# Keys and values of the context: made in the second layer's collecting stage instead of between its experts

## The reference

```python
def grouped_experts(xf, expert_id, gates, w_gu, w_down):
    ...
    def expert_block(args):
        xb, e = args
        a, b = jnp.split(xb @ w_gu[e], 2, axis=-1)
        return (jax.nn.silu(a) * b) @ w_down[e]
    ...
    return jax.ops.segment_sum(y_rows[dest] * w_sorted[:, None], tok_sorted, num_segments=T)
...
def c_mixer(u, uc, in_w, out_w, rpb, need_ctx):
    def proj(t):
        q, k, v, z = jnp.split(t @ in_w, 4, axis=-1)
        ...
    q, k, v, z = proj(u)            # 512 tokens
    q_c, k_c, v_c, z_c = proj(uc)   # 256 rows of context
    o = neighbourhood_latent(q, k, v, k_c, v_c, rpb)
    y = (o * jax.nn.silu(z)) @ out_w
```

## Time and profile before

| | us |
|---|---|
| median of 3 runs | 2964.3 (2963.15 to 2972.04) |
| the profiled execution, its own time | 2958.89 |
| its span, first to last instruction | 2957.1 |
| PE busy | 2686.4 (91%) |
| DVE / ACT / POOL busy | 1140.6 / 640.4 / 289.8 |
| second layer's experts, first to last product of PE | 1538.8 to 2054.5 |
| collecting stage, SP's first load to the next stage's first product | 2061.5 to 2099.2 |
| its first transpose on PE | 2092.1 |

### The profile page before, as it was taken

How to read it: one execution, slowest core, us unless ns; L and a number is a source line. 1 busy time by engine, 2 the same in 40 slices (tenths; PEclk the granted TensorE clock), 3 DMA queues, 4 the chain that set the end, 5 groups by cost and what they waited for, 6 DMA issues and landing times.

```text
span 2957.1 us, 35044 instructions
## 1 busy us (share of the span) xinstructions
PE 2686.4 (91%) x14222; PEld 1738.8 (59%) x14222; DVE 1140.6 (39%) x2541; ACT 640.4 (22%) x1316; POOL 289.8 (10%) x280
## 2 busy tenths in 40 slices
PE   7999979999999699999979989997699998999998
PEld 5858743554444476776743444443577667865864
DVE  4344441112122544424341111110755455665566
ACT  2130421123222100100020010000353341043053
POOL 2002000111110000001000111110200001212211
PEclk9999989999999899999989999999899999999999
DMA  5603248999998521232378999997310111320310
GB/s 182 263 10 136 115 183 353 417 414 414 378 417 364 212 86 63 80 126 101 133 289 363 421 420 420 416 419 329 124 45 31 66 38 57 97 82 14 112 26 36
DMA packets 115354, 610.19 MB, mean 206 GB/s; under 512 B 13148, under 2 KB 25500, under 8 KB 88432
## 3 DMA queue, kind: packets, MB, share of 16 engines
q1 hardware_dynamic: 92000, 541.98, 46.0%
q0 software_dynamic: 20512, 54.76, 5.5%
q10 hardware_dynamic: 2672, 11.09, 1.0%
HBM read 588.84 MB, written 35.65 MB: 211 GB/s over the span
## 4 chain that ended last, share of the span: by engine, by line
PE 74%; DMA 11%; DVE 6%; PEld 3%; issue 2%; ACT 2%; POOLq 0%; PEldq 0%; SPq 0%; DVEq 0%; ACTq 0%; POOL 0%
PE psum L689 24%; PE psum L2172 12%; PE psum L2184 6%; DMA ring<-in_expert_w_gu 6%; PE psum L818 6%; PE psum L944 5%; PE psum L589 4%; DMA arena<-in_expert_w_gu 4%; PE psum L973 3%; PE psum L962 3%; PE psum L579 2%; PE psum L1239 2%; PEld psum L689 2%; PE psum L2165 1%; PE psum L2178 1%
## 5 line engine op out<-in xcount | busy, mean ns | idle before, releaser
L2172 PE MATMUL psum<-ring,XT 128*64 128x512 f32 x1024 | 242.1, 612 | 24.1 <-DMA ring<-in_expert_w_gu 21.1
L2172 PE MATMUL psum<-arena,XT 128*64 128x512 f32 x1024 | 237.9, 608 | 15.7 <-DMA arena<-in_expert_w_gu 15.6
L2243 DVE TENSOR_TENSOR XT<-XT,psum 64x512 f32<-64x512 f32 x64 | 44.1, 690 | 529.5 <-ACT XT L2246 529.5
L689 PE MATMUL psum<-arena 128*128 128x256 f32 x1056 | 238.7, 379 | 0.0
L689 PEld LDWEIGHTS psum<-arena 128*128 128x128 f32 x1056 | 200.3, 190 | 27.1
L944 PE MATMUL psum<-arena 64*128 64x384 f32 (+7 forms) x736 | 187.4, 473 | 27.1 <-ACT arena L998 16.2
L689 PE MATMUL psum<-XT,ring 128*128 128x256 f32 x864 | 195.3, 380 | 5.3 <-DVEq L3250 5.3
L689 PEld LDWEIGHTS psum<-XT,ring 128*128 128x128 f32 x864 | 163.3, 190 | 32.2 <-issue 6.8
L2172 PEld LDWEIGHTS psum<-ring,XT 128*64 128x64 f32 x1024 | 74.8, 140 | 168.5 <-issue 129.6
L818 PE MATMUL psum<-ring,arena 128*128 128x512 f32 x384 | 166.6, 593 | 4.4 <-DVEq L3250 2.0
L2172 PEld LDWEIGHTS psum<-arena,XT 128*64 128x64 f32 x1024 | 76.7, 139 | 154.5 <-issue 131.7
(11 more groups left out here) (382 smaller groups left out, 3779.2 us busy)
## 6 DMA issues: line engine op xcount, KB each, us to landing
ring<-in_expert_w_gu SPq DMA_DIRECT2D x64, 2048.0 KB, 19.1
arena<-in_expert_w_gu SPq DMA_DIRECT2D x64, 2048.0 KB, 20.3
arena<-in_expert_w_down SPq DMA_DIRECT2D x32, 2048.0 KB, 13.6
ring<-in_expert_w_down SPq DMA_DIRECT2D x32, 2048.0 KB, 12.5
ring<-in_ada_w SPq DMA_DIRECT2D x12, 2048.0 KB, 8.5
ring<-in_fox_w_in SPq DMA_DIRECT2D x8, 2048.0 KB, 12.8
ring<-in_ret_w_in SPq DMA_DIRECT2D x8, 2048.0 KB, 10.5
ring<-in_c_in_w SPq DMA_DIRECT2D x8, 2048.0 KB, 7.7
```

Source lines behind the costliest of these rows:

```text
L689: m = pe.matmul(ps[0][:, 2 * P * i:2 * P * (i + 1)], x, w, start=(not onto and i == 0 and c == 0), stop=(c == 3), skip_group_check=True)
L2172: i = pe.matmul(psum[side * BR:(side + 1) * BR, 0:FF], x[:, 4 * part + c, :], w[:, c, side * FF:(side + 1) * FF], start=(part == 0 and c = ...
```

## The change

The 16 jobs of `self.last` leave the experts and become the first thing that PE does in the collecting stage. In detail:

- `shares` no longer names `self.last`. POOL loads the first two of the eight units as before, while the experts run, and the other six in `late_weights`, at the start of its part of `cb1`, ahead of its update of `H`.
- `late_pe` puts all 16 jobs ahead of the transposes of `cb1`. They rotate over PSUM banks 1, 6 and 7.
- All 16 are drained by ACT, four of them ahead of the squares of each row tile (`late_act`).
- Both stores (`context_k_c`, `context_v_c`) are issued by ACT at the end of its part of `cb1`, which then waits for them as before.
- The gain is loaded at expert 20 into the lane's region. `YG`, `Z` and `ROWS` move to columns that don't overlap `XC`, the weight buffers, the keys and the values.

```diff
-                        side = "av"[n]
+                        side = "a"
...
             def shares(self):
-                return (self.out, 5, 13), (self.last, 15, 31)
+                return (self.out, 5, 13),
+
+            def weights_used(self, pool): pass
+
+            def late_weights(self, pool):
+                for j in self.last.jobs:
+                    if j["release"] and j["units"][0] + 2 < self.u1:
+                        ContextWeights.load(pool, j["units"][0] + 2)
+                super().weights_used(pool)
+
+            def late_pe(self, pe):
+                self.last.pe(pe)
+                self.last.all_taken(pe)
+
+            def late_act(self, act, first=0, last=None):
+                self.last.drains(act, "a", first, last)
...
-                self.last.pe(pe, *in_share(e, 15, 31, 16))
...
-                self.last.drains(act, "a", *in_share(e, 15, 31, 16))
-                if e == 23:
...
-                    act.dma_start(context_k_c, self.KC_).then_inc(self.s("kept"), 16)
+                if e == 20:
+                    act.dma_start(self.GAIN, io["norm_final"].partition_broadcast(P)).then_inc(self.s("gain"), 16)
...
-            def finished(self, act):
+            def finished(self, act): pass
+
+            def stored(self, act):
                 self.last.all_taken(act)
+                act.dma_start(context_k_c, self.KC_).then_inc(self.s("kept"), 16)
                 act.dma_start(context_v_c, self.VC).then_inc(self.s("kept"), 16)
-
-            def stored(self, act):
                 act.wait_ge(self.s("kept"), 32)
...
             def act(self, act):
-                act.dma_start(self.G, io["norm_final"].partition_broadcast(P)).then_inc(self.s("gain"), 16)
+                jobs = len(self.lane.last.jobs)
                 for t in range(NT):
+                    self.lane.late_act(act, jobs * t // NT, jobs * (t + 1) // NT)
...
             def pool(self, pool):
+                self.lane.late_weights(pool)
                 pool.wait_ge(*self.till("rstd", 1))
...
             def pe(self, pe):
+                self.lane.late_pe(pe)
                 for t0 in range(0, NT, 2):
```

More of the change, by code:

```diff
@@ L1955, in build @@
             TMP, ROWS, JUNK = region(W0 + 4096, 2, 256), region(W0 + 4608, NCT, D), region(W0 + 6656, D)
-            KC_, VC = region(W0 + 2048, KC, CTX), region(W0, NCT, D)
+            KC_, VC, GAIN = region(W0 + 2048, KC, CTX), region(W0, NCT, D), region(W0 + 6656, D)
             def jobs(self):
@@ L1986, in jobs @@
                     for t in range(NCT):
-                        side = "av"[t]
+                        side = "a"
                         p.job(side, mm_R(u, 0, KC, 256, 0, 256, self.XC, t, CW), copy_out(side, self.VC[:, t, 256 * m:256 * (m + 1)]),
@@ L2017, in act @@
                     self.norm_out_act(act)
-                self.last.drains(act, "a", *in_share(e, 15, 31, 16))
-                if e == 23:
-                    for j in self.last.jobs[0:8]:
-                        self.last.taken(act, j)
-                    act.dma_start(context_k_c, self.KC_).then_inc(self.s("kept"), 16)
+                if e == 20:
+                    act.dma_start(self.GAIN, io["norm_final"].partition_broadcast(P)).then_inc(self.s("gain"), 16)
             def dve(self, dve, e, part):
@@ L2038, in dve @@
                     self.norm_out_dve(dve)
-                self.last.drains(dve, "v", *in_share(e, 15, 31, 16))
-            def finished(self, act):
+            def finished(self, act): pass
+            def stored(self, act):
                 self.last.all_taken(act)
+                act.dma_start(context_k_c, self.KC_).then_inc(self.s("kept"), 16)
                 act.dma_start(context_v_c, self.VC).then_inc(self.s("kept"), 16)
-            def stored(self, act):
                 act.wait_ge(self.s("kept"), 32)
@@ L2348, in build @@
             kind = "combine"
-            YG = region(0, NT, 2, D)
+            YG = [region(2 * D * t, 2, D) for t in range(NT)]
             def __init__(self, tag, lane):
@@ L2363, in sp @@
                 for t in range(NT):
-                    sp.dma_start(self.YG[:, t, :, :], rows[:, t, :, :]).then_inc(self.s(f"got{t}"), 16)
+                    sp.dma_start(self.YG[t], rows[:, t, :, :]).then_inc(self.s(f"got{t}"), 16)
         class CombineNorm(Combine):
@@ L2389, in dve @@
                     for k in range(2):
-                        i = dve.scalar_tensor_tensor(H[:, t, :], self.YG[:, t, k, :], gates[:, k, t:t + 1], H[:, t, :], ALU.mult, ALU.add)
+                        i = dve.scalar_tensor_tensor(H[:, t, :], self.YG[t][:, k, :], gates[:, k, t:t + 1], H[:, t, :], ALU.mult, ALU.add)
                         if k == 0:
@@ L2420, in build @@
         class CombineNorms(Combine):
-            Z, ROWS = region(2 * NT * D, NT, D), region(NT * D, NT, D)
-            G, JUNK = region(12288, D), region(13312, D)
+            YG = [region(at, 2, D) for at in (6144, 12288, 14336, 16384)]
+            Z, ROWS = region(8192, NT, D), region(12288, NT, D)
+            JUNK = region(ContextLane.W0 + 4608, D)
             one, two = slice(0, NT), slice(NT, 2 * NT)
             def act(self, act):
-                act.dma_start(self.G, io["norm_final"].partition_broadcast(P)).then_inc(self.s("gain"), 16)
+                jobs = len(self.lane.last.jobs)
                 for t in range(NT):
+                    self.lane.late_act(act, jobs * t // NT, jobs * (t + 1) // NT)
                     act.wait_ge(*self.till("summed", t + 1))
@@ L2445, in dve @@
             def dve(self, dve):
-                dve.wait_ge(self.s("gain"), 16)
+                dve.wait_ge(self.lane.s("gain"), 16)
                 for t in range(NT):
@@ L2454, in dve @@
                     dve.wait_ge(*self.till("summed", t + 1))
-                    dve.tensor_tensor(self.Z[:, t, :], H[:, t, :], self.G, ALU.mult).then_inc(self.s("weighted"), 1)
+                    dve.tensor_tensor(self.Z[:, t, :], H[:, t, :], self.lane.GAIN, ALU.mult).then_inc(self.s("weighted"), 1)
                 dve.wait_ge(self.s("weighted"), NT)
```

## The result

The changed kernel takes 2994.02 us (median of five runs, 2991.07 to 3004.88) against 2964.3 of before: 29.7 us more. The ratio is 1.010, with a 95% interval of 1.0087 to 1.0113. The forecast was 2996. Its profiled execution has a span of 2991.5 us, 34.4 more than before, of which 4.1 lie ahead of the second layer's experts (first product at 1542.9 instead of 1538.8), where the change does nothing.

What follows compares the result with a forecast made beforehand. The prediction took transfers to bound the experts, with PE idle 30.6 us in the collecting stage. Experts -18, collecting stage +40.6 and stores with slow products +9.2 gave +31.8 us on 2964.3, so 2996, range 2982 to 3016.

Steps and rivals of the forecast that it cites:

- The experts are limited by bytes: Second layer's experts: transfers, not PE, set the pace at 15.6 us an expert; 18 us less, including the tail.
- some 4: Changed kernel's experts: PE would wait some 4 us in each expert for transfers.
- a lighter tail of 2 us: End of the experts: PE without jobs frees slots sooner, so less DMA time stays unused; 2 us gained.
- The jobs: Collecting stage: 16 jobs take 56.8 us, plus 2 for the low clock and 3 for late weights.
- my 0 and 10: Collecting stage: lateness of the third weight unit, from nothing late at best to 10 us at worst; 3 taken.
- the free case: Late weight loads where little else ran: two issued together landed after 6.0 and 8.0 us, against 17.2 beside the experts.
- The cost of at most 2 us: Collecting stage: late weight unit sharing with 2.6 KB packets gets half the rate, costing at most 2 us.
- The chain behind the last job: Collecting stage: last drain 0.5 us, then squares to first transpose 8.9 us, now serial.
- The stores: Behind the transposes: both stores land in 7.5 us, ACT's drain holds PE; with slow first products 9.2 us added.
- POOL: Collecting stage: POOL's update of `H`, now behind the weight loads, takes 13.4 us from the factors and stays hidden.
- The second rival: Experts: PE falls to the low clock between waits, the gain of 18 becomes 0, total 3014; 9 in 100.
- The third: Collecting stage: late units not hidden, PE held 10 us three times, 30 us instead of 3, total 3023; 5 in 100.

Runs made afterwards that it cites:

- a_squares_first: The changed kernel with ACT taking each row tile's squares ahead of its quarter of the drains; 2984.42 us, ratio 1.0064 to before.
- b_one_matmul: The kernel before, each of the 16 jobs issuing one matmul instead of 8, all loads, drains and stores kept; 2965.58 us, ratio 1.0006.
- b_two_units: The kernel before, all jobs using two ready weight units, six later loads left out, keys' store behind the last expert; 2946.9 us, ratio 0.9942.
- a_both: The changed kernel with squares ahead of drains and both stores right behind the last job's drain; 2979.97 us, ratio 1.0048 to before.
- a_stores_early: The changed kernel with the keys' store issued after job 8 and the values' after the last job, before the last squares; 2992.52 us, ratio 1.0090.
- split_12: a_both with 12 of the 16 jobs between the experts again and four late; 2955.74 us, ratio 0.9970 to before.
- split_8: a_both with eight jobs between the experts and eight late; 2962.63 us, ratio 0.9988 to before.

## Why the prediction was right, point by point

- *The experts are limited by bytes.* Shown from both sides: bytes away, PE kept, -17 us; PE away, bytes kept, 0. The size, 18, was measured as 17.1. The bytes were right (15.5 us an expert for 15.6). PE waited 2.7 us in each expert and not some 4, since part of its products ran at the low clock. What I had called a lighter tail of 2 us was partly something else: 1.3 us came behind the last expert. The values' store no longer runs beside the last scatter to `y_dram`, which landed after 2.6 us instead of 4.9. From PE's last product to SP's first load it takes 4.6 to 5.9 us in the nine kernels with no store there, 7.0 and 6.9 with one (before, b_one_matmul), and 10.4 with two (b_two_units).
- *The jobs.* 56.8 + 2 + 3 us were 55.7 + 3.8 + 4.4. A job takes 3.48 us, not 3.55, and the low clock was paid twice, at the start and behind the wait: a wait in a row of products costs more than its length. The wait of 4.4 lies between my 0 and 10. The unit landed after 10.5 us, the next after 9.3, beside SP's loads, and the later ones in 6 us: between the two rows, nearer to the free case, as taken. The cost of at most 2 us, which the prediction worked out from packet sizes, was too low.
- *The chain behind the last job.* 9.4 forecast, 9.1 from the last drain to the transposes. That it is the order of ACT's queue and nothing deeper, a_squares_first showed.
- *The stores.* Direction and releaser right, size wrong: 7.5 us of added wait forecast, 4.2 measured. The term assumed that the stores are issued after the last write to `XT` and that the second adds its full transfer time. They were issued at 2126.5, ahead of ACT's last write at 2127.2, and landed after 3.9 and 6.0 us. That wait, again, costs clock behind it: 2.5 us, 1.7 forecast.
- *POOL.* Its update of `H` ran from 2120.4 to 2132.2 and the next stage's first product came at 2133.0. It was hidden; that stage doesn't wait for POOL, which a_both shows.
- *The second rival* (low clock eats the gain) had its premise, a granted clock of 0.94 and waits that bring it down, and not its consequence. *The third* (every late unit waited for) did not occur: one wait, not three.

The misses by stage are +0.9 in the experts, +1.9 up to the first transpose (+2.1 in the jobs), -3.3 at the stores and +0.8 for the clock behind them. They cancel within 1 us, and the spread of single profiles is larger than that: that the sum came out so close is partly luck.

## What to carry to other kernels

Work of a busy engine is free in a stage that is limited by transfers, and what it is worth to move it away is its bytes, not its time; test it by keeping one and leaving the other out. Before filling a gap, measure it, and put in what fits; then look at each queue that the work passes: here a drain ahead of the last reduction made a wait of 9 us, and stores at the end of a stage made one of 6 us for PE. A transfer moved off the path may fall beside one that was just hidden.

## What the runs showed of the hardware

- TensorE's clock can fall after waits much shorter than the 3.7 us of the earlier trace rows, but the length of the last wait alone doesn't tell whether it does. Four rows of PE's timeline in the changed kernel's experts (16 of these matmuls take 3.65 us at full clock, 32 take 7.09):

```profile
1762.32 5.35 PE L2183 MATMUL psum<-arena,XT 128*64 128x512 f32 x16 [2.50 <-DMA arena<-in_expert_w_gu]
...
1778.62 3.65 PE L2183 MATMUL psum<-ring,XT 128*64 128x512 f32 x16 [0.24 <-DMA ring<-in_expert_w_gu]
...
1903.40 3.65 PE L2183 MATMUL psum<-ring,XT 128*64 128x512 f32 x16 [2.05 <-DMA ring<-in_expert_w_gu]
...
1919.17 8.79 PE L2183 MATMUL psum<-arena,XT 128*64 128x512 f32 x32 [1.63 <-DMA arena<-in_expert_w_gu]
```

  The products after 1.63 us were slow, those after 2.05 us were not. The section "HAM oscillation" of "TensorE: Matmul & The Clock Gate" in the Trainium skill describes products between waits for transfers, where each burst starts at the low clock. This case agrees for part of the bursts, as the rows show. In a stage that the transfers limit it cost little: at most some 3 us of 500 by the profiles compared above.
- A 1 MB store from SBUF landed in 3.8 us alone (the values' store of a_stores_early), in 4.5 beside the experts' last scatter (before), in 5.2 beside one late load, and in 12.4 beside the experts' stream. Two issued together landed in 3.9 and 6.0, and in 7.4 and 9.3 in split_12, where SP's loads were still in flight. The experts' last scatter to `y_dram` landed after 4.9 us beside one store (before, b_one_matmul) and after 2.4 to 3.3 with none (after, split_12, split_8). The next stage's first load came 1 to 2 us later beside one store and some 5 later beside two (b_two_units).
